# A two-block transformer kernel on one Trainium2 core: ScalarE's table sets asked for by name, squares of the feed-forward's norms added on VectorE before TensorE sums them, and one bank read moved forward

## The reference, cut to what matters

```python
# first block
h = rms_norm(x, norm_mix_g)
log_f = log_sigmoid(f_logit + b_f)                    # exp and ln of 8 rows
p = softmax(...)                                      # 8 heads, blocks of 128 queries
x = x + (g_conv * y_conv + g_attn * y_attn) @ w_o
h = rms_norm(x, norm_ffn_g)                           # the feed-forward's norm
up = causal_dwconv(h @ w_up, conv_ffn_w)              # 5632 columns
a, b = split(up)
x = x + (silu(a) * b) @ w_down
x = rms_norm(x, norm_f_g)                             # and then, in the second block,
u = _rms_norm(concat(meta, x), norm_pre[0])
# second block, mixer 1, for each of 32 heads
a = sigmoid(a0 + ...); decay = exp(-exp(w))
kk = kk / norm(kk)                                    # a root, as exp(-0.5 ln)
y = (y - mean) * rsqrt(var + GN_EPS)                  # another
y = (...) * silu(g)
# mixer 2: norm_post, norm_pre, norms of q and kv, attention, silu gate, norm_post
```

## Time and profile before

| | before |
|---|---|
| median of 3 runs | 2391.45 us (2390.91 to 2392.31) |
| the profiled execution's own time | 2393.26 us |
| its span, first to last instruction | 2391.5 us |
| PE busy | 2307.8 us, 96% |
| DVE, ACT, POOL busy | 50%, 38%, 48% |
| granted TensorE clock, mean | 0.987 |

### The profile page before, as it was taken

One profiled execution on the slowest core, in us unless ns is written; L12 is line 12 of the kernel. 1 busy time (PEld: TensorE's weight loads), 2 busy tenths in 40 slices (PEclk: granted clock), 3 DMA queues, 4 the chain that ended last, 5 costly groups with the idle time before them and its releaser, 6 DMA issues.

```text
span 2391.5 us, 51950 instructions
## 1 busy us (share of the span) xinstructions
PE 2307.8 (96%) x22099; PEld 1794.6 (75%) x22099; DVE 1206.5 (50%) x2267; ACT 907.9 (38%) x1808; POOL 1144.5 (48%) x771
## 2 busy tenths in 40 slices
PE   8999999899999899999999999999799999999898
PEld 7788787788887677777777777777689787777776
DVE  3353265577801655555555555555420576556521
ACT  4122112333302355555555555555320443433300
POOL 4555575876663433333444444333446344343345
PEclk9999999999999999999999999999799999999999
DMA  3333232233322222222222222221523331121212
GB/s 110 89 80 80 80 95 72 85 100 97 108 98 63 81 66 66 66 66 66 71 69 66 66 66 73 67 66 56 181 63 115 98 80 49 51 60 42 91 55 95
DMA packets 263758, 188.07 MB, mean 79 GB/s; under 512 B 18267, under 2 KB 242393, under 8 KB 263145
## 3 DMA queue, kind: packets, MB, share of 16 engines
q1 hardware_dynamic: 263529, 184.76, 25.8%
HBM read 162.69 MB, written 22.04 MB: 77 GB/s over the span
## 4 chain that ended last, share of the span: by engine, by line
PE 87%; POOL 4%; DVE 3%; issue 2%; ACT 1%; DMA 1%; SPq 1%; POOLq 0%; DVEq 0%; ACTq 0%
PE ps L1323 18%; PE ps L158 15%; PE ps L159 14%; PE ps L160 14%; PE ps L1485 3%; PE ps L1501 3%; PE ps L1527 2%; PE ps L2358 2%; POOL w_lo L149 2%; PE ps L1474 1%; PE ps L1441 1%; PE ps L1413 1%; PE ps L1336 1%; PE ps L220 1%; PE ps L2344 1%
## 5 line engine op out<-in xcount | busy, mean ns | idle before, releaser
L149 POOL TENSOR_TENSOR w_lo<-raw,w_hi 128x1024 fp32r<-128x1024 f32 (+1 forms) x196 | 494.4, 2522 | 16.4
L146 POOL TENSOR_SCALAR w_hi<-raw 128x1024 fp32r<-128x1024 f32 (+1 forms) x196 | 218.5, 1115 | 567.0 <-PE ps L160 547.1
L158 PE MATMUL ps<-h_hi,w_hi 128*128 128x512 f32 x616 | 243.5, 395 | 7.6 <-POOL w_lo L149 7.0
L160 PE MATMUL ps<-h_hi,w_lo 128*128 128x512 f32 x616 | 240.2, 390 | 0.0
L159 PE MATMUL ps<-h_lo,w_hi 128*128 128x512 f32 x616 | 239.8, 389 | 0.0
L1855 POOL TENSOR_TENSOR kp<-k_b,kp 128x528 f32<-128x528 f32 x16 | 29.6, 1848 | 351.2 <-ACT kp L1622 351.2
L1323 PE MATMUL ps<-mixed_r,raw 128*64 128x264 f32 x1024 | 154.1, 390 | 4.7 <-ACT g_b L1564 4.7
L158 PEld LDWEIGHTS ps<-h_hi,w_hi 128*128 128x128 f32 x616 | 115.8, 188 | 33.3 <-POOL w_lo L149 9.6
L1323 PE MATMUL ps<-mixed_k,raw 128*64 128x264 f32 x1024 | 138.4, 390 | 0.0
L160 PEld LDWEIGHTS ps<-h_hi,w_lo 128*128 128x128 f32 x616 | 115.6, 188 | 24.7
L159 PEld LDWEIGHTS ps<-h_lo,w_hi 128*128 128x128 f32 x616 | 115.8, 188 | 23.0
(11 more groups left out here) (444 smaller groups left out, 5916.6 us busy)
## 6 DMA issues: line engine op xcount, KB each, us to landing
raw<-in_rwkv_w_in_dram SPq DMA_DIRECT2D x64, 512.0 KB, 4.1
raw<-in_w_up_dram SPq DMA_DIRECT2D x44, 512.0 KB, 3.9
raw<-in_w_in_dram SPq DMA_DIRECT2D x41, 512.0 KB, 3.8
raw<-in_w_down_dram SPq DMA_DIRECT2D x22, 512.0 KB, 3.5
raw<-in_mla_w_in_dram SPq DMA_DIRECT2D x22, 512.0 KB, 3.9
sb_kept<-xT SPq DMA_DIRECT2D x16, 528.0 KB, 2.7
xT<-sb_kept SPq DMA_DIRECT2D x16, 528.0 KB, 4.4
raw<-in_rwkv_w_out_dram SPq DMA_DIRECT2D x16, 512.0 KB, 4.0
```

Source lines behind the costliest of these rows:

```text
L146: nc.gpsimd.tensor_scalar(w_hi[s][:, 0:width], raw[s][:, 0:width], 1.0, 0.0, ALU.mult, ALU.add).then_inc(split_hi, 1)
L149: nc.gpsimd.tensor_tensor(w_lo[s][:, 0:width], raw[s][:, 0:width], w_hi[s][:, 0:width].bitcast(F32), ALU.subtract).then_inc(split_ready, 1)
L158: nc.tensor.matmul(dst, w[0], x[0], start=start, stop=False)
L160: return nc.tensor.matmul(dst, w[1], x[0], start=False, stop=stop)
```

## The change

It has three parts.

2. VectorE adds squares before TensorE sums them. For the feed-forward's norm tiles 0 to 6 become one (`ffn_add`, six adds), and TensorE does 2 sums for 8, inside `up_unit` 0 before its seventh tile. At the end, sum u is 3 matmuls for 8 (five `u_add` between the residual adds), sum v is 2 for 8 (six adds behind them, in front of `uT`), all behind the last down unit. `xg_low` of a tile now stands in that tile's own turn.
3. `late_out` 0 stands directly behind the wait for the root, `late_out` 1 behind the fifth `y`.

```diff
-        def ffn_sum(pe, j):
-            pe.wait_ge(sq_ready, j + 1)
-            mm = nc.tensor.matmul(ps[:, 6, :], ones[:], norm_ffn.sq[:, j, :], start=(j == 0), stop=(j == KD - 1))
-            if j == KD - 1:
-                mm.then_inc(sq_summed, KD)
+        def ffn_sum(pe):
+
+            pe.wait_ge(f_added, KD - 2)
+            nc.tensor.matmul(ps[:, 6, :], ones[:], norm_ffn.sq[:, 0, :], start=True, stop=False)
+            pe.wait_ge(sq_ready, KD)
+            nc.tensor.matmul(ps[:, 6, :], ones[:], norm_ffn.sq[:, KD - 1, :], start=False, stop=True).then_inc(sq_summed, KD)
...
                 if n == 0:
+                    if k == KD - 2:
+                        ffn_sum(pe)
                     pe.wait_ge(h_lo_ev, KD + k + 1)
...
-                if e == 0:
-                    norm_sum(pe, 0, m)
...
+        def norm_sums(pe):
+
+            pe.wait_ge(x2_done, 2)
+            pe.wait_ge(u_added, KD - 3)
+            nc.tensor.matmul(ps[:, 4, :], ones[:], sq_v[:, X2_ORDER[0], :], start=True, stop=False)
+            for p in (KD - 2, KD - 1):
+                pe.wait_ge(e_sq, 2 * p + 1)
+                mm = nc.tensor.matmul(ps[:, 4, :], ones[:], sq_v[:, X2_ORDER[p], :], start=False, stop=(p == KD - 1))
+            mm.then_inc(e_sum, 1)
+            pe.wait_ge(v_added, KD - 2)
+            nc.tensor.matmul(ps[:, 5, :], ones[:], xT[:, X2_ORDER[0], 0:T1], start=True, stop=False)
+            pe.wait_ge(e_sq, 2 * KD)
+            nc.tensor.matmul(ps[:, 5, :], ones[:], xT[:, X2_ORDER[KD - 1], 0:T1], start=False, stop=True).then_inc(e_sum, 1)
...
-            for j in range(KD - 1):
-                ffn_sum(pe, j)
-            up_unit(pe, 0)
-            ffn_sum(pe, KD - 1)
-            for n in range(1, 2 * KF):
+            for n in range(2 * KF):
                 up_unit(pe, n)
...
+            norm_sums(pe)
...
+            nc.scalar.preload_act_table_set(LOG_EXP)
             act.wait_ge(unit_done, 1)
...
+            nc.scalar.preload_act_table_set(LOG_EXP)
             for j in range(KD):
...
-            nc.scalar.activation(wa_in[:, 0:1], eps_col[:, 2:3], ACT.Ln)
+            nc.scalar.preload_act_table_set(LOG_EXP)
...
+            nc.scalar.preload_act_table_set(SIGMOID)
             act.wait_ge(lo_used, 1)
...
             for m in range(8):
                 dve.wait_ge(unit_done, U_O + m + 1)
                 nc.vector.tensor_tensor(xT[:, m, 0:T1], xT[:, m, 0:T1], ps[:, 4 + m % 2, :], ALU.add).then_inc(x1_done, 1)
-                if m:
-                    xg_low(dve, m - 1)
-            xg_low(dve, 7)
+                if m >= 2:
+                    ffn_add(dve, m - 1)
+                xg_low(dve, m)
             nc.vector.memset(up_raw[:, :, 0:2], 0.0).then_inc(up_lo, 1)
             dve.wait_ge(up_lo, 1)
             dve.wait_ge(rs_ready, norm_ffn.n0 + 1)
+            late_out(dve, 0)
             for j in range(KD):
                 nc.vector.scalar_tensor_tensor(out=norm_ffn.y[:, j % 4, 0:T1], in0=xT[:, j, 0:T1], scalar=prm("g_ffn", j),
                                                in1=norm_ffn.r[:, 0:T1], op0=ALU.mult, op1=ALU.mult).then_inc(y_ready, 1)
                 if j:
                     h2_low(dve, j - 1)
-                if j in (2, 6):
-                    late_out(dve, j // 4)
+                if j == 4:
+                    late_out(dve, 1)
             h2_low(dve, 7)
...
                 nc.vector.tensor_tensor(x2T[:, m, :], xT[:, m, 0:T1], ps[:, m, :], ALU.add).then_inc(x2_done, 1)
+                if 2 <= p < KD - 1:
+                    u_add(dve, p - 1)
+            for p in range(1, KD - 1):
+                dve.wait_ge(e_sq, 2 * p + 2)
+                if p >= 2:
+                    dve.wait_ge(v_added, p - 1)
+                acc = xT[:, X2_ORDER[0], 0:T1]
+                nc.vector.tensor_tensor(acc, acc, xT[:, X2_ORDER[p], 0:T1], ALU.add).then_inc(v_added, 1)
             dve.wait_ge(x2_done, KD)
             dve.wait_ge(meta_step, 6)
             dve.wait_ge(e_r, 2)
...
+        def u_add(dve, p):
+
+            dve.wait_ge(e_sq, 2 * p + 1)
+            if p >= 2:
+                dve.wait_ge(u_added, p - 1)
+            acc = sq_v[:, X2_ORDER[0], :]
+            nc.vector.tensor_tensor(acc, acc, sq_v[:, X2_ORDER[p], :], ALU.add).then_inc(u_added, 1)
+
+        def ffn_add(dve, j):
+
+            dve.wait_ge(sq_ready, j + 1)
+            if j >= 2:
+                dve.wait_ge(f_added, j - 1)
+            nc.vector.tensor_tensor(norm_ffn.sq[:, 0, :], norm_ffn.sq[:, 0, :], norm_ffn.sq[:, j, :], ALU.add).then_inc(f_added, 1)
...
             def exponents():
+                nc.scalar.preload_act_table_set(LOG_EXP)
                 act.wait_ge(scanned, i + 1)
                 act.wait_ge(pa, 13 * i + PA["lx"])
                 nc.scalar.activation(e_in[:], lsum[:], ACT.Exp, scale=DECAY).then_inc(fa, 1)
...
             def logs():
+                if not A:
+                    nc.scalar.preload_act_table_set(LOG_EXP)
                 if A:
                     act.wait_ge(ssk_out, i + 1)
                     nc.scalar.activation(rn_b, rn_b, ACT.Ln).then_inc(fa, 1)
...
                 if Cs:
                     act.wait_ge(gn_ln, c + 1)
                     nc.scalar.activation(ysq_b, yb_b, ACT.Exp, scale=-0.5).then_inc(gn_r, 1)
+                if A:
+                    nc.scalar.preload_act_table_set(SIGMOID)
...
                 all_passes(act, pass_act)
+                nc.scalar.preload_act_table_set(LOG_EXP)
                 norm_post0.act(act, lambda e, j: e.wait_ge(m_out, j + 1))
```

More of the change, by code:

```diff
@@ L21 @@
 KD = D // P
+LOG_EXP, SIGMOID = "natural_log_exp_and_others", "sigmoid_and_others"
 T1 = 512
@@ L405, in program @@
         x1_done = sem("x1_done")
+        f_added, u_added, v_added = sem("f_added"), sem("u_added"), sem("v_added")
         up_w2, taps, up_gate, up_step, up_hi, up_lo = (sem(n) for n in ("up_w2", "taps", "up_gate", "up_step", "up_hi", "up_lo"))
@@ L555, in down_unit @@
                 mm.then_inc(unit_done if m == 3 else x2_mm, 1)
-                if e == 0:
-                    norm_sum(pe, 0, m)
-        def norm_sum(pe, which, p):
-            pe.wait_ge(e_sq, 2 * p + which + 1)
-            pe.wait_ge(x2_done, which + 1)
-            src = xT[:, X2_ORDER[p], 0:T1] if which else sq_v[:, X2_ORDER[p], :]
-            mm = nc.tensor.matmul(ps[:, 4 + which, :], ones[:], src, start=(p == 0), stop=(p == KD - 1))
-            if p == KD - 1:
-                mm.then_inc(e_sum, 1)
+        def norm_sums(pe):
[10 more added lines that the diff above has]
+            nc.tensor.matmul(ps[:, 5, :], ones[:], xT[:, X2_ORDER[KD - 1], 0:T1], start=False, stop=True).then_inc(e_sum, 1)
         def lora_pe(pe):
@@ L680, in front_pe @@
                 down_unit(pe, q)
-            for p in range(4, KD - 1):
-                norm_sum(pe, 0, p)
-            norm_sum(pe, 1, 0)
-            norm_sum(pe, 1, 1)
-            norm_sum(pe, 0, KD - 1)
-            for p in range(2, KD):
-                norm_sum(pe, 1, p)
+            norm_sums(pe)
             lora_pe(pe)
```

## The result

The changed kernel took 2376.32 us (median of 4 executions, 2373.65 to 2379.18), the kernel before 2391.47: ratio 0.9934, interval 0.9922 to 0.9946. That is 15.1 us less, inside the range and on the forecast's side, and 5.8 us more than the 2370.5 predicted. The profiled execution (2373.65 us, span 2371.9) has the shortest time of the four and gained 19.6 us of span; the others were 2373.72, 2378.93 and 2379.18.

What follows compares the result with a forecast made beforehand. TensorE, busy 96% of the span, was taken as the bound, so only less TensorE work or shorter waits help. Terms 1.3 + 8.0 + 6.0 + 3.1 + 1.3 + 1.3 = 21.0 us off 2391.45 gave 2370.5, range 2365 to 2379.

Steps and rivals of the forecast that it cites:

- Front: Kernel start: forget gate's logarithm and first softmax lose a load each, shortening waits for `q_main` and `a_p`; 1.3 us.
- Feed-forward's norm: Fewer TensorE sums and an earlier root bring the fifth up unit forward, limited by VectorE's chain; 8.0 us.
- End norms: Norms at the end: 11 sums fewer, less new idle time before sum v, bring `lora_pe` forward; 6.0 us.
- half of 1.6: End norms: allowance for TensorE's clock perhaps falling in the idle time before sum v; a full fall costs 1.6 us.
- Pass 0: End of pass 0: earlier exponents' load takes 2.4 us off the 4.7 wait, plus 0.7 for a kept clock; 3.1 us.
- Behind the passes: After pass 15: DMA wait and residual between the mixers each gain 1.3 us from a removed load.
- Passes: Steady passes: no gain while TensorE stays full, and GpSimd's earlier products cost nothing; 0 us.
- Rivals 1 and 4: Steady passes: GpSimd catches VectorE, scan slips 0.4 us a pass (2376.5, chance 0.13) or 1.8 us (2397, chance 0.03).
- Rival 2: Loads asked for by name don't shorten waits: stall sits elsewhere or another input is late; 2378.8, chance 0.06.
- Rival 3: Table switches cost a drain of about 1.38 us beside the 1.28 load; up to 8 us more, 2362; chance 0.04.
- the last step: Whole kernel: from profiled span to median, taking the median as 1.8 us under profiled time, as before; gives 2370.5.
- signs of being wrong: A pass growing 0.2 us or more, late-bank waits over 4 us in all, or TensorE's clock low through `lora_pe`.

Runs made afterwards that it cites:

- again: The changed kernel run once more with no edit; five executions from 2374.02 to 2379.80 us, the profiled one 2379.41 us.
- banks: The changed kernel with late bank reads spread out (behind the third, fifth and eighth y); median 2373.86 us, ratio 0.9922 to the kernel before.
- loads_only: The kernel before with only the change's eight table-set preload calls added; median 2384.36 us, ratio 0.9964.
- loads_2: Second run of the kernel before with only the table sets asked for by name; median 2386.80 us over seven executions.
- squares_only: The kernel before with only the squares added ahead on VectorE at both norms, no preloads or moved bank reads; median 2384.15 us, ratio 0.9967.
- vsplit: The changed kernel with sum v shared out otherwise: VectorE adds four tiles, not six, TensorE does 4 matmuls for 2; median 2375.11 us, ratio 0.9924.
- both: The changed kernel with late bank reads spread out and sum v shared out otherwise, together; median 2370.29 us, ratio 0.9910 to the kernel before.

## Why the prediction was right, and where it was off

Measured place by place, in the profile of before and the first of the change:

| place | predicted | measured | how |
|---|---|---|---|
| up to the first up unit | 1.3 | 1.1 | 378.82 - 377.72 |
| feed-forward's norm | 8.0 | 6.7 | 34.49 - 27.81 |
| from there to `lora_pe` | 6.0 | 7.0 | 359.92 - 352.96 |
| `lora_pe` to pass 1 | 3.1 | 2.4 | 53.27 - 50.91 |
| pass 1 to the end of the `z_kept` wait | 1.3 | 1.7 | 886.84 - 885.17 |
| from there to the residual | 1.3 | 1.6 | 144.96 - 143.39 |
| behind it | 0 | -0.7 | 533.2 - 533.9 |
| sum | 21.0 | 19.6 | spans 2391.5 - 2371.9 |

- **Front.** 1.1 agrees by luck. From the first `w_in` unit to the first up unit there are 354.27 us before and 354.17 after; the rest (1.0) is that the fp32 matmuls with `x_diag` took 9.20 us for 10.17 in this execution, and in `again` they took 10.14. The wait for `q_main` is gone (0.6), that for `a_p` stayed at 0.8: no load stood on its way. In its place comes 0.27 for a `w_lo`, which the sums used to cover. The term should have been 0.1 to 0.4.
- **Feed-forward's norm.** The root came as worked out: 384.58 + 0.63 = 385.21 is 7.5 us behind the start of the stage, predicted 386.2 - 378.8 = 7.4. The term was mis-sized in VectorE's chain: from the root to `late_out` 2 it took 404.74 - 385.21 = 19.5 us where 16.3 + 2.2 = 18.5 was put. The pair at 385.95 is held 2.5 us, the rows at 392.52 and 398.64 2.2 and 1.5, and two more `h_lo` took 1.52 for 0.68. Of the 6.7 that were measured, 1.5 are the clock, which fell behind the 2.35 wait before and stayed up here; the prediction had them in, since it counted 5.44 us for every unit. And I had spread the wait over two units at a microsecond or two each; it came as one of 2.76 and one of 0.94. `banks` shows that 2.4 us of it were a matter of order at this place. What the load taken from the root is worth here was not run by itself; in `loads_only` it was worth nothing.
- **End norms.** `uT` stands 756.53 - 751.35 = 5.2 us behind the last residual add, predicted 764.8 - 759.7 = 5.1. `lora_pe` 7.14 behind it, predicted 6.8. The idle time before sum v is 2.43 for 2.4. The clock stayed up there in the first profile and fell in that of `again`, for 1.7 us: the "half of 1.6" that I took is the middle of what is really one or the other, and 0.8 of the 1.0 that the term measured too much. The prediction's two ways to the term don't agree either: 6.7 by the times of `lora_pe`, 9.5 - 2.4 = 7.1 by the work taken off, and the second was the nearer. The rest lies ahead of the last residual add: 348.96 us from the fifth up unit to it before, 345.82 after, 3.1 less for sums of 2.6.
- **Pass 0.** The wait fell from 4.70 to 2.33, predicted 2.3. The 0.7 for a kept clock did not come: the clock falls there in every profiled execution, only for longer or shorter.
- **Behind the passes.** 1.7 and 1.6 for 1.3 and 1.3, where a load is 1.28. The wait for the DMA shows 2.5 less, which overstates it, and is why the wait came out at 3.7 and not near 5.0: TensorE was slower ahead of it (granted clock over the 30 us ahead of the wait 0.60 for 0.66), and arrived later.
- **Passes.** 0 as predicted. From the same matmul of one pass to that of the next it is 57.47 us in before, in the change and in `loads_only`, with a 57.6 here and there. Rivals 1 and 4 fall. In `again` it is 57.50.
- **Rival 2** (loads give nothing) falls with `loads_only` at four of its places and holds at one: the waits for `q_main`, `g_b`, `z_kept` and the residual are gone or shorter, those for the late banks are not. **Rival 3** (2.66 us for a switch) falls too: Ln to Exp went from 1.31 us apart to 0.03, so a switch cost 1.28. The Trainium skill, *ScalarE: Activation LUTs*, section "What ACT_TABLE_LOAD costs", gives a drain of about 1.38 us besides; no place measured here shows it.

So the mechanisms were right but for the load at the feed-forward's root, whose gain is not shown, and the terms were off by 1.4 of the 5.8 us. (The upper ends of the terms add up to 25.0 and not 25.2.) The other 4.4 stem from the last step, which took over from before that the median lies 1.8 us under the profiled execution. The change's profiled execution has the mean clock of before's (0.987) but is the shortest of its four, with the median 2.7 above it. A sum made from one profile silently holds its clock fixed, and the change's other executions are up to 6 us longer, with a lower mean clock in all that are longer than 2376 us. One of the prediction's own signs of being wrong came in this way: the clock was low at the start of `lora_pe` in the profile of `again`, and in neither of the change's other two. What is shown: the same kernel with the same waits at both norms has it fall at four places in one execution and not, or for less, in another. What stays open: which circumstance decides it from execution to execution, whether the chip has a part in it, why `loads_only`, that has neither of the new waits, scatters most, and which places the executions without a profile lost at.

## What to carry to other kernels

Take a gain of a few microseconds in a kernel bound by TensorE as a gain in waits plus a lottery in clock: measure ten executions, not three, and where two versions cost the same take the one that leaves TensorE no gap of 2 us. Read a stage's gain together with its granted clock: in `loads_only` a gain of 1.5 us that looked like the saved load was the clock. When additions are moved from TensorE to VectorE, leave TensorE as many as fit into the time in which it must wait for the root anyway. Naming a table set ahead is worth the load (1.28 us) where TensorE waits behind the switch and no other engine is late, and nothing elsewhere: of 45 loads, four paid nearly in full (two at pass 0, one behind pass 15, one at the residual), those at the front together 0.1 to 0.4 us, and that at the feed-forward's root nothing in `loads_only`.

## What was not expected of the hardware

- The clock fell near 50 us in five of the twelve profiled executions (`again`, `loads_2`, `squares_only`, `vsplit`, `both`: 0.89 over the window from 45 to 60 us), with TensorE never idle there. What stands ahead are 2.4 us of small matmuls on 16 partitions (47.65 to 50.02 in the first profile). In the others the same instructions left it at 1.00.
- The same fp32 matmuls at the start (`x_diag`, 64) took 9.20 us in one execution of the changed kernel and 10.14 in another, behind the same wait of 0.97. What differs is when they speed up: from 18 to 20 us the first has 19 of them and the other 12, from 20 to 22 us 20 and 18. The clock column reads 1.00 in all these windows, so it doesn't show this. In six of the twelve profiled executions there are 9.7 us or more from their start to the first `w_in` unit, and the five with the low clock near 50 us are among these.
- A lower clock is given back in part or wholly where a wait for another engine comes behind it: 0.94 us shrinks to nothing at the fifth up unit, and the wait of 1.65 for a `w_lo` near 460 us is gone, with no time lost.
